# First stage of a hybrid block: x times g by channels for three token blocks, the norm's factor at eviction

## The reference, cut to what matters

```python
hn = rms_norm(h, mix_norm_g)          # x * rsqrt(mean(x*x) + EPS) * g, per token
proj = hn @ w_in                      # [1040, 1024] @ [1024, 6656]
rq, rk, rv, rg, sq, sk, sv, gr, gs = split(proj)
y_ret = rms_norm(retention(rq, rk, rv), ret_norm_g) * silu(rg)
y_swa = sliding_window_attention(sq, sk, sv, q_norm_g, k_norm_g, sinks)
h = h + (sigmoid(gr) * (y_ret @ w_ret) + sigmoid(gs) * (y_swa @ w_swa)) @ w_out
h = h + square(relu(rms_norm(h, mlp_norm_g) @ w_up)) @ w_down
```

## Time and profile before

| | |
|---|---|
| median of 3 runs | 1615.72 us (1615.67 to 1616.56) |
| the profiled execution: its time, its span | 1615.03 us, 1613.1 us |
| PE busy | 1603.3 us (99%) |
| first product of the first stage starts | 9.34 us |
| first product of the next stage's main part starts | 63.25 us |

### The profile page before, as it was taken

One profiled execution on the slowest core, in us unless ns is written; L12 is line 12 of the kernel. 1 busy time (PEld: TensorE's weight loads), 2 busy tenths in 40 slices (PEclk: granted clock), 3 DMA queues, 4 the chain that ended last, 5 costly groups with the idle time before them and its releaser, 6 DMA issues.

```text
span 1613.1 us, 22668 instructions
## 1 busy us (share of the span) xinstructions
PE 1603.3 (99%) x7984; PEld 1340.3 (83%) x7984; DVE 1038.1 (64%) x1977; ACT 769.6 (48%) x1567; POOL 425.7 (26%) x611
## 2 busy tenths in 40 slices
PE   8999999999999999999999999999999999999999
PEld 6888888888888888888888888888888888888887
DVE  6775556655657787766554338866665656766675
ACT  6533334544547777762122126655555544444442
POOL 1001010221238898874211000122112222100000
PEclk9999999999999999999999999999999999999999
DMA  8323231645436566668553223354444389633452
GB/s 282 125 97 117 98 124 66 239 149 190 163 110 159 158 176 167 159 159 267 167 187 111 66 78 118 126 174 151 144 144 155 120 316 358 240 96 98 153 180 92
DMA packets 128815, 253.31 MB, mean 157 GB/s; under 512 B 14928, under 2 KB 50176, under 8 KB 128704
## 3 DMA queue, kind: packets, MB, share of 16 engines
q1 hardware_dynamic: 82656, 124.81, 24.8%
q0 software_dynamic: 45904, 126.93, 23.5%
q10 hardware_dynamic: 144, 0.13, 0.0%
HBM read 157.05 MB, written 69.47 MB: 140 GB/s over the span
## 4 chain that ended last, share of the span: by engine, by line
PE 93%; DMA 2%; DVE 2%; POOL 1%; ACT 1%; issue 0%; SPq 0%; DVEq 0%; ACTq 0%
PE bank L1089 29%; PE bank L1094 28%; PE bank L1093 28%; PE bank L1375 2%; PE bank L1407 1%; PE bank L1389 1%; DMA RT<-YA 1%; DMA XCH<-in_x_ch 0%; POOL PR L966 0%; PE bank L1132 0%; PE bank L1507 0%; PE bank L1293 0%; PE bank L1424 0%; PE bank L1457 0%; DVE WL L2177 0%; PE bank L1411 0%
## 5 line engine op out<-in xcount | busy, mean ns | idle before, releaser
L1089 PE MATMUL bank<-WH,ADH 128*128 128x512 f32 x448 | 174.3, 389 | 0.0
L1093 PE MATMUL bank<-WH,ADL 128*128 128x512 f32 x448 | 174.3, 389 | 0.0
L1094 PE MATMUL bank<-WL,ADH 128*128 128x512 f32 x448 | 174.3, 389 | 0.0
L1089 PE MATMUL bank<-HN,WH 128*128 128x512 f32 x384 | 152.9, 398 | 0.1
L966 POOL TENSOR_SCALAR PR<-PR,RC 128x272 f32<-128x272 f32 (+1 forms) x128 | 139.3, 1228 | 47.4 <-DVE RC L2672 47.2
L2103 ACT CAST ADH<-ARAW 128x512 fp32r<-128x512 f32 x112 | 69.5, 621 | 169.9 <-PE bank L1094 156.7
L1094 PE MATMUL bank<-HN,WH 128*128 128x512 f32 x384 | 150.2, 391 | 0.0
L1093 PE MATMUL bank<-HN,WL 128*128 128x512 f32 x384 | 150.1, 391 | 0.0
L2926 DVE TENSOR_TENSOR ADL<-ARAW,ADH 128x512 fp32r<-128x512 f32 x112 | 77.5, 692 | 97.1 <-ACT ADH L2103 97.1
L1089 PE MATMUL bank<-SOPH,WH 128*128 128x512 f32 x256 | 99.8, 390 | 0.0
L1093 PE MATMUL bank<-SOPH,WL 128*128 128x512 f32 x256 | 99.6, 389 | 0.0
(11 more groups left out here) (356 smaller groups left out, 4200.6 us busy)
## 6 DMA issues: line engine op xcount, KB each, us to landing
ARAW<-uop SPq DMA_DIRECT2D x112, 256.0 KB, 3.1
uop<-US POOLq DMA_DIRECT2D x64, 256.0 KB, 2.8
WRAW<-in_w_up SPq DMA_DIRECT2D x15, 1024.0 KB, 6.3
PW<-PR SPq DMA_DIRECT2D x56, 272.0 KB, 3.0
RAW<-in_w_in SPq DMA_DIRECT2D x58, 256.0 KB, 4.1
gates<-TB POOLq DMA_DIRECT2D x48, 256.0 KB, 2.7
uop<-UA POOLq DMA_DIRECT2D x48, 256.0 KB, 3.2
proj<-SA POOLq DMA_DIRECT2D x36, 256.0 KB, 2.5
```

The costliest lines, as they stand in the source:

```text
L1089: mm = pe.matmul(bank, ahi, bhi, start=first, stop=False, skip_group_check=onto)
L1093: pe.matmul(bank, alo, bhi, start=False, stop=False, skip_group_check=onto)
L1094: return pe.matmul(bank, ahi, blo, start=False, stop=last, skip_group_check=onto)
```

## The change

Blocks 0, 1 and 2 enter the first product as x times g, not normed: `XCH` gets their x by channels first (half blocks of 256 KB for 0 and 1), x times g is made in place (the first half block on DVE, the rest on POOL, `make_xg`), ACT casts it (`XGH`), DVE subtracts (`XGL`), and the factor is applied at eviction as the scale of an ACTIVATE. PE takes blocks 0 and 1 in turn, two steps k of each, and then block 2. The PE transposes of g and of blocks 0 and 1 are gone, and so are the two copies to `SR`.

The normed operand is now made for all 8 blocks in one way, in the order 3, 4, 5, 6, 7, 0, 1, 2 (`SEQ`, place p): SP loads `XCH` again for place p, POOL multiplies by g (`make_xs`, two 128x512 multiplies a block), PE spreads the factors (`factors_row` at the places of `ROWS`), DVE multiplies by the factors (`scale_x`, two operations), ACT casts, DVE subtracts. Statistics are taken in the order `STAT`, all `XR` loads are POOL's. `GBC` is issued after the last XCH load; `PX` and `RAW` follow without the former wait, `PY` waits for block 2's end.

```diff
+FIRST = 3
+SEQ = (3, 4, 5, 6, 7, 0, 1, 2)
+STAT = (3, 0, 4, 1, 5, 2, 6, 7, NB)
+MAKE_META = 5
...
+            LATE_XG = {1: (1, 0), 3: (0, 1), 4: (1, 1)}
+            load_xg(0, 0)
             load_slab(0, w_cols(w_in, 0))
-            for b in range(2, NB):
...
+            sp.dma_start(XCH[:, 2, :, :], x_ch[2]).then_inc(xc_full[2], 16)
+            for p in range(NB):
+                if p < 3:
+                    sp.wait_ge(hn_lo, max(XG_AT[p, 0], XG_AT[p, 1]))
+                else:
+                    sp.wait_ge(xs_rdy, 1 + 2 * (p - 2))
+                sp.dma_start(XCH[:, p % 3, :, :], x_ch[SEQ[p]]).then_inc(xc_full[p % 3], 16)
             sp.dma_start(GBC[0:META, :], g_mix[0:META, :]).then_inc(g_full, 16)
...
+            def times_g(tile, u):
+                gain = GCH[:, 4 * u:4 * u + 4].unsqueeze(2).to_broadcast([P, 4, P])
+                pool.tensor_tensor(tile, tile, gain, ALU.mult).then_inc(xg_rdy, 1)
...
+            for pair in range(KT // 2):
+                for b in range(2):
+                    for k in (2 * pair, 2 * pair + 1):
+                        first_step(b, k)
+            ROWS = {(2, 1): 0, (3, 0): 1, (3, 5): 2, (4, 3): 3, (5, 1): 4, (5, 6): 5, (6, 4): 6, (7, 2): 7}
...
+                if b < FIRST:
+                    act.wait_ge(rstd_rdy, STAT_AT[b] + 1)
+                    act.activation(TB[:, b % 2, :], first_bank(b)[:, :], ACT.Copy, scale=RSTD[:, b:b + 1]).then_inc(a_free, 1)
...
+            for p in range(NB):
+                scale_x(p)
+                if p < 4:
+                    invert(SEQ[p + 1])
+                if p < NB - 1:
+                    factors(SEQ[p + 1])
+                if p == 4:
+                    invert(NB)
+                lo_x(SEQ[p])
+                if p < 2:
+                    invert(p + 1)
+                elif p == 4:
+                    norm_meta()
```

More of the change, by code:

```diff
@@ L582, in build @@
         pst_a, pst_b, PSA0, PSB0 = out_done, h1_ld, 16 * 12 * NSG, 16 * 4 * NSG
-        rt_full, RT0 = x_full, 32
-        kv_full, KV0 = x_full, 64
+        rt_full, RT0 = x_full, [48, 32, 32, 32]
+        kv_full, KV0 = x_full, [RT0[i] + 32 for i in range(4)]
         GS0, CF0, MU0 = 4, 48, 64
@@ L1185, in tokens @@
                 return lambda k: (pair[0][:, k, b * P:(b + 1) * P], pair[1][:, k, b * P:(b + 1) * P])
[L1187 to L1200, removed]
             def keep_warm(count):
@@ L1206, in keep_warm, with xg_block @@
                     pe.matmul(B[1][:, 0:2 * P], WARM[:, 0:P], WARM[:, 0:2 * P], start=True, stop=True)
[L1208 to L1221, removed]
-                for k in range(KT):
[L1223 to L1227, removed]
+            def xg_block(b):
+                return lambda k: (XGH[:, b, k, :], XGL[:, b, k, :])
@@ new lines, in _ @@
+            pe.wait_ge(eps_set, 1)
+            keep_warm(4)
+            for pair in range(KT // 2):
[3 more added lines that the diff above has]
+            ROWS = {(2, 1): 0, (3, 0): 1, (3, 5): 2, (4, 3): 3, (5, 1): 4, (5, 6): 5, (6, 4): 6, (7, 2): 7}
+            for b in range(2, NB):
+                if b == 4:
+                    pe.wait_ge(a_free, 1)
+                elif b > 4:
+                    pe.wait_ge(a_free, b - 1)
+                for k in range(KT):
+                    first_step(b, k)
+                    if (b, k) in ROWS:
+                        factors_row(ROWS[b, k])
+                    if (b, k) == (6, 6):
+                        transpose_meta()
@@ L2225, in _, with factors, norm_meta @@
-            norm_x(0)
-            split_lo(0, 0)
-            lo_x(0, (0,))
-            for k in range(1, 4):
-                split_lo(0, k)
-            lo_x(0, (1,))
+            def factors(b):
+                dve.wait_ge(rstd_rdy, STAT_AT[b] + 1)
+                dve.tensor_scalar(DG[:, AT[b] % 2, :], IDN[:, :], RSTD[:, b:b + 1], None, ALU.mult).then_inc(xn_rdy, 1)
+            def norm_meta():
+                dve.wait_ge(rstd_rdy, STAT_AT[NB] + 1)
+                dve.wait_ge(g_full, 16)
+                dve.scalar_tensor_tensor(out=ST[0:META, :], in0=XR[0:META, STAT_AT[NB] % 4, :], scalar=RSTD[0:META, NB:NB + 1],
+                                         in1=GBC[0:META, :], op0=ALU.mult, op1=ALU.mult).then_inc(xn_rdy, 1)
@@ new lines, in lo_xg, with lo_x @@
+            def lo_xg(b, u):
+                dve.wait_ge(hn_hi, XG_AT[b, u])
+                ks = slice(4 * u, 4 * u + 4)
+                dve.tensor_tensor(XGL[:, b, ks, :], xg_cols(b, u), XGH[:, b, ks, :].bitcast(F32), ALU.subtract)\
+                   .then_inc(hn_lo, 1)
+            def lo_x(b):
+                for u in range(2):
+                    dve.wait_ge(hn_hi, hi_at(b, u))
+                    dve.tensor_tensor(x_part(b, u, 1), x_cols(b, u), x_part(b, u, 0).bitcast(F32), ALU.subtract)\
+                       .then_inc(hn_lo, 1)
@@ new lines, in scale_x @@
+            def scale_x(p):
+                dve.wait_ge(xt_full, row_at(p))
+                for u in range(2):
+                    dve.wait_ge(xg_rdy, NXG - 1 + 2 * p + u + 1)
+                    dve.tensor_tensor(x_cols(SEQ[p], u), xs_cols(p, u),
+                                      B[6 + p % 2][:, 0:P].unsqueeze(1).to_broadcast([P, 4, P]), ALU.mult).then_inc(xs_rdy, 1)
+            dve.wait_ge(gc_full, 16)
+            dve.wait_ge(x0_full, 16)
+            dve.tensor_tensor(xg_cols(0, 0), xg_cols(0, 0), GCH[:, 0:4].unsqueeze(2).to_broadcast([P, 4, P]), ALU.mult)\
+               .then_inc(xs_rdy, 1)
```

360 lines of the change are left out of this document (195 added, 165 removed).

## The result

The changed kernel takes 1619.14 us (median of 8 runs, 1618.55 to 1624.01) against 1615.41 us (8 runs, 1614.46 to 1616.56) of the kernel before on the same chip: ratio 1.0028, 95% interval 1.0017 to 1.0039. It is slower by 3.7 us in the medians, a little over the 0.2% that the prediction took as the least that can be told from no change; the prediction said 1617.0, and its range held the time.

What follows compares the result with a forecast made beforehand. TensorE bounds the kernel (busy 1603.3 of 1613.1 us). A stage end of 56.1 us without new waits plus 8.4 of waits gives 64.5, 1.25 later than before: 1617.0 us, likeliest range 1613.5 to 1620, with rivals 1611 to 1623.

Steps and rivals of the forecast that it cites:

- the end: Next stage's first main product on TensorE, at 63.25 us before; forecast 64.5, wrong if before 60 or after 67.
- its likeliest case: The forecast and the small gains: end within 3.2 us of before, time 1613.5 to 1620 us; chance 0.52.
- wait 3: TensorE ahead of the third factors' row, by the same statistics loads one round on: 0.8 us.
- wait 4: TensorE ahead of the fourth factors' row, for block 6's factor, whose XR load stands behind GpSimd's multiplies: 2.05 us.
- wait 1: TensorE ahead of block 1's first step, for its first half's load, multiply, cast and low part: 1.3 us.
- wait 2: TensorE ahead of block 3, the first normed operand, for a late statistics load, square and casts: 0.9 us.
- wait 5: Fifth factors' row: VectorE and ScalarE need 5.3 us between diagonals, TensorE comes after 4.3: 0.95 us.
- wait 6: Seventh factors' row: block 1's diagonal stands behind the normed meta tile, which waits for GBC: 2.05 us.
- GpSimd the bound: Slower rival: 2.2 us multiplies as VectorE and GpSimd interfere; end 70.2, 1622.7 us; chance 0.28, including all waits larger.
- The faster rival: GpSimd's loads and the meta tile not late, multiply 0.9 to 1.2 us: end 58.3, 1610.8 us; chance 0.14.
- felt at the start alone: Rival: first product 3.1 us earlier, later waits the old ones; end 60.2, 3.1 earlier; chance 0.06.
- wait 7: End of the stage: next stage's weights' low parts, behind more VectorE work than before: 0.35 us.

Runs made afterwards that it cites:

- the run with all places and g on GpSimd: Changed kernel with GBC's load first, factors' rows later, squares ahead of casts, statistics loads 5 and 6 ahead of GpSimd's multiplies; 1618.3 us.
- GBC early: Changed kernel with GBC's load issued ahead of the normed blocks' XCH loads instead of behind them; 1618.0 us.
- the rows later: Changed kernel with TensorE's factors' rows at later places between the products, nothing else; 1619.8 us.
- the best version with g on GpSimd: The run with all places and g on GpSimd, plus earlier statistics loads 3 and 4, small loads last, next weights earlier, VectorE's splits before last sums; 1616.4 us.
- g on VectorE: Changed kernel with the eight normed blocks' multiply by g moved from GpSimd into VectorE's scaling; 1621.4 us.
- small loads late: Changed kernel with GpSimd's three small loads (COLS, SLI, SK) issued after the stage's last store instead of ahead of the fifth XR load; 1622.2 us.
- in sequence: Version with all four places altered and g on VectorE (1614.6 us), with blocks 0 and 1 one after the other instead of in turn; 1616.9 us.

## Why the prediction was right, and where its sizes were off

The range held the time, but the end is at the rim of what the prediction allowed: 66.89, where it called itself wrong from 67 on, and 3.64 us later than before, where its likeliest case went to 3.2. And the total is nearer than its parts, which is luck: wait 3 was 2.2 us too short and the slow products were missing, while wait 4 was 1.95 too long. By its own steps, the idle time worked out from the distances of the rows above, less 0.696 a step and 0.14 a row:

| step | forecast, us | measured, us |
|---|---|---|
| first product | 6.2 | 6.83 |
| wait 1, blocks 0 and 1 | 1.3 | 1.4, elsewhere |
| wait 2, block 3 | 0.9 | 0.5 |
| wait 3, third row | 0.8 | 3.0 |
| slow products | none | 1.6 |
| wait 4, fourth row | 2.05 | 0.1 |
| wait 5, fifth row | 0.95 | 0.65 |
| wait 6, seventh row (GBC) | 2.05 | 2.3 |
| sixth row, wait 7 and the rest | 0.35 | 0.6 |
| end | 64.5 | 66.89 |

- **The mechanism was right in the main.** The start gained, and later waits took more than it gave: late statistics loads that GpSimd issues (waits 2 to 4), the chain of scaling, cast, square and diagonal (5), GBC (6). Wait 6 was also tested by itself and held; so was GpSimd's part in waits 3 and 4, by taking its multiplies away.
- **Wait 1 came out in size, not in place.** The forecast had it ahead of block 1's first step, behind the low part XGL. In this execution that step (9.01) has no marked wait; 0.65 us are lost at block 0's second step, behind VectorE's second split of the weights, and the rest in small pieces. Where GpSimd's first multiply began later (6.93, in the run with all places and g on GpSimd), two splits took 1.29 us and the wait was the forecast one, 1.18 us behind XGL.
- **The first product** was 0.6 later. 0.5 of that is g: VectorE's multiply began at 4.01, when g's 4 KB had landed (3.2 us from an issue at 0.81), where I had put 3.5 for both loads. From that multiply to the first product it is 2.82 us here, and also with GBC early, with the rows later and in the best version with g on GpSimd, while the multiply itself began between 3.92 and 4.21.
- **Wait 3 was mis-sized, by 2.2 us**: I reckoned it from wait 2's load one round on, and so with 5.4 us for the load of block 5's statistics; it took 8.2. In the forecast each load's time was a number from before, and the prediction took the stretch from 18 us on for emptier than before. In the changed kernel SP sends its loads by channels as early as their buffers come free, and both streams meet at 383 to 424 GB/s from 26 to 30 us. That this alone makes them slow does not fit the rates: block 5's load took 8.2 us through a stretch of 119 GB/s, and 5.4 in the best version with g on GpSimd, where the queues moved 258 to 348 from 21 to 26 us. What sets a load's duration here stays open. Another 0.35 us of wait 3 are the diagonal, 0.64 us beside GpSimd's multiply instead of 0.29. The same holds for wait 4: block 6's load was issued 2 us earlier than forecast (28.39), took 8.1 us instead of 4.3, and landed 1.8 later (36.5).
- **Wait 4 and the slow products** are one: the fourth row's diagonal was ready at 38.86 and TensorE's slow products ended there. The three executions of the changed kernel with a mean clock of 1.000 took 1618.9 to 1619.2 us, which is its median, so the slow products as such added nothing to that.
- **GpSimd's multiply** was quicker than forecast (1.02 quiet, 1.22 in the mean, for 1.5), and the rival "GpSimd the bound" fell by its own condition (from 1.85 us on). The Trainium skill's ratio ("GPSIMD Engine Reference", section 3.1) gave an estimate of 1.35 us, which is nearer. The Trainium skill's other rule ("SBUF — State Buffer", section "Who interferes with whom") bears on VectorE more than I used it: two subtractions took 3.68 us beside GpSimd's multiplies, against 1.29 with g on VectorE. The trace agrees with its direction: GpSimd's slowest single multiply was 2.0 us and VectorE's subtraction 1.84 each.
- **The faster rival** had its first condition met: the multiply took 1.22 us, and GpSimd issued block 6's load 2 us earlier than forecast. It fell all the same, since the loads took longer.
- **The rival "felt at the start alone"** fell with the first late load.

What stays open: 0.5 us of the span's growth lie behind this stage, and I did not follow them.

## What to carry to other kernels

Work saved at the start of a chain is worth only what the next waits leave: list what comes after by issue time of its loads, and take a load's duration as a range, not as one median: the same 512 KB for the statistics took from 4.9 us (changed kernel) to 9.7 (small loads late). Moving arithmetic to the engine that also issues loads delays these loads and slows the other engine's two-operand work; nearly the same order with the multiply in VectorE's fused scaling was 3.7 us quicker. An early start pays only once order and loads behind it are redone too: here 1613.8 us against 1619.1 for the change alone, and even that is not clear of the 1615.1 before.

## What was unexpected of the hardware

TensorE's granted clock fell to half (1.2 GHz) behind idle times of 1.4 to 3.0 us within this stage, and not always: it stayed at 1.00 behind 2.07 us (small loads late) and fell behind 1.92 (g on VectorE). In 5 of 8 executions of the changed kernel the mean clock of the whole run is below 1.000 (0.999 to 0.996, the last with 1624.01 us), in 4 of 5 with g on VectorE, in 2 of 11 in sequence, and in none of the 27 of before in one comparison, whose longest wait in the stage is 1.08 us. The changed kernel's times spread over 5.5 us, before's over 2.1. That the clock makes this spread is not shown: with g on GpSimd in the best version the four executions below 1.000 are the four slowest, but with GBC early the fastest (1616.41) is one of them, at 0.997.

The granted clock does not tell all either. With GBC early it is 1.00 from 7 to 11 us, and yet TensorE's products began every 0.43 us from 7.4 to 10.4, as at half clock.
